# The first weights of the condition in four column steps, a selection product in place of transposes, and three projection tiles fed slice by slice

## The reference, cut to what matters

```python
def adaln(cond, w, b):
    m = jax.nn.silu(cond) @ w + b
    return jnp.split(m.reshape((-1, 1, N_MOD * D_MODEL)), N_MOD, axis=-1)
...
sh_m, sc_m, g_m, sh_f, sc_f, g_f = adaln(c, ada_w[l], ada_b[l])
csh_m, csc_m, ... = adaln(c_ctx, ada_w[l], ada_b[l])
h_ctx = modulate(rmsnorm(ctx, norm_mix_w[l]), csh_m, csc_m)   # h * (1 + scale) + shift
pc = split_in(h_ctx @ w_in[l])                                # forget gates and values of the context
h = modulate(rmsnorm(x, norm_mix_w[l]), sh_m, sc_m)
pl = split_in(h @ w_in[l])                                    # q, two forget gates, v, g, u, sv, two merge gates
```

## Time and profile before

| | us |
|---|---|
| median of 3 executions | 1562.19 (1561.62 to 1562.67) |
| the profiled execution | 1561.22 |
| its span in the profile | 1559.4 |
| busy PE, DVE, ACT | 1201.3, 562.7, 419.7 |
| share of DMA in the chain that ended last | 54% |

### The profile page before, as it was taken

How to read it: one execution, slowest core, us unless ns; L and a number is a source line. 1 busy time by engine, 2 the same in 40 slices (tenths; PEclk the granted TensorE clock), 3 DMA queues, 4 the chain that set the end, 5 groups by cost and what they waited for, 6 DMA issues and landing times.

```text
span 1559.4 us, 18602 instructions
## 1 busy us (share of the span) xinstructions
PE 1201.3 (77%) x8124; PEld 732.3 (47%) x8124; DVE 562.7 (36%) x827; ACT 419.7 (27%) x542; POOL 29.5 (2%) x36
## 2 busy tenths in 40 slices
PE   4999999997656657556656656756666899999997
PEld 1878899943311112111111111111111689999997
DVE  3788776511101101101101101101101597777566
ACT  3676656221100000000000000000000455367544
POOL 0002000000000000000000000000000000000000
PEclk9999999999888877878878878788878899999999
DMA  9546858599999999999999999999999855555551
GB/s 363 203 159 219 304 206 338 197 391 429 419 429 428 427 428 428 428 428 427 428 428 427 428 428 428 427 429 427 429 428 428 303 162 163 161 189 186 180 180 50
DMA packets 118719, 520.90 MB, mean 334 GB/s; under 512 B 7264, under 2 KB 85088, under 8 KB 90736
## 3 DMA queue, kind: packets, MB, share of 16 engines
q1 hardware_dynamic: 118496, 519.64, 83.3%
q10 hardware_dynamic: 144, 0.09, 0.0%
HBM read 518.66 MB, written 1.05 MB: 333 GB/s over the span
## 4 chain that ended last, share of the span: by engine, by line
DMA 54%; PE 33%; DVE 6%; ACT 3%; issue 2%; SPq 1%; DVEq 0%; ACTq 0%
DMA pair<-in_wu 27%; PE B L1652 14%; DMA pair<-in_wd 13%; DMA pair<-in_wg 11%; PE B L1656 7%; DMA wslot<-in_w_in 4%; PE B L2010 3%; DVE wslot_r L931 2%; PE B L2054 1%; PE B L1743 1%; PE B L1628 1%; ACT whi L506 1%; PE B L1974 1%; PE B L1949 0%; SPq L381 0%
## 5 line engine op out<-in xcount | busy, mean ns | idle before, releaser
L2010 PE MATMUL B<-pair,xs 128*32 128x512 f32 x2048 | 315.9, 745 | 203.8 <-DMA pair<-in_wu 126.3
L2010 PEld LDWEIGHTS B<-pair,xs 128*32 128x32 f32 x2048 | 63.3, 123 | 424.8 <-issue 178.3
L2054 PE MATMUL B<-pair,hidT 128*32 128x512 f32 x1008 | 166.2, 792 | 104.1 <-DMA pair<-in_wd 95.1
L2054 PEld LDWEIGHTS B<-pair,hidT 128*32 128x32 f32 x1008 | 31.9, 129 | 218.4 <-DMA pair<-in_wd 145.6
L931 DVE TENSOR_TENSOR wslot_r<-wslot,whj 128x2048 fp32r<-128x2048 f32 x52 | 118.8, 2288 | 31.4 <-ACT whj L506 31.4
L1652 PE MATMUL B<-hnh,whj 128*128 128x256 f32 x496 | 122.7, 285 | 0.4 <-ACT whj L506 0.4
L506 ACT ACTIVATE whj<-wslot 128x2048 fp32r<-128x2048 f32 x51 | 97.3, 1912 | 89.9 <-PE B L1656 84.2
L1652 PE MATMUL B<-hn_r,whj 128*128 128x256 f32 x496 | 121.5, 283 | 0.0
L1251 DVE SCALAR_TENSOR_TENSOR x<-B,mod,x 128x256 f32<-128x256 f32 x128 | 55.9, 479 | 149.5 <-PE B L1992 149.5
L1282 DVE COPY ye<-B 128x512 f32<-128x512 f32 x15 | 10.4, 692 | 273.5 <-PE B L2054 273.5
L1271 DVE TENSOR_TENSOR hid<-sgm,B 128x512 f32<-128x512 f32 x16 | 11.0, 688 | 262.7 <-PE B L2010 262.7
(11 more groups left out here) (475 smaller groups left out, 1821.0 us busy)
## 6 DMA issues: line engine op xcount, KB each, us to landing
pair<-in_wg SPq DMA_DIRECT2D x64, 2048.0 KB, 41.5
pair<-in_wu SPq DMA_DIRECT2D x64, 2048.0 KB, 40.9
pair<-in_wd SPq DMA_DIRECT2D x62, 2048.0 KB, 41.0
wslot<-in_w_in SPq DMA_DIRECT2D x58, 1024.0 KB, 5.2
aslot<-in_ada_w SPq DMA_DIRECT2D x20, 1024.0 KB, 7.4
wslot<-in_ada_w SPq DMA_DIRECT2D x4, 1024.0 KB, 9.2
wslot<-in_w_out SPq DMA_DIRECT2D x4, 1024.0 KB, 8.3
wslot<-in_wa SPq DMA_DIRECT2D x4, 1024.0 KB, 5.1
```

What stands on the lines that cost most here:

```text
L2010: mm = e.matmul(B[b][32 * j:32 * j + 32, :], XS[x // 8][:, k, 32 * (x % 8):32 * (x % 8) + 32], tile_at_page(t)[:, 512 * j:512 * j + 512], ...
L2054: mm = e.matmul(B[3 + db][32 * r:32 * r + 32, :], hidT[:, 128 * c + 32 * j:128 * c + 32 * j + 32], v2(tile_at_page(t + c // 2))[:, c % 2, ...
```

## The change

- The condition's 8 MB are loaded by columns: four steps s of 256 shift columns (t = 0) and 256 scale columns (t = 1), each 1 MB in runs of 1 KB. After a step the shift and scale of slices 2s and 2s+1 are complete.
- x is loaded first, then the identity, step 0, tile 0, ctx, step 1, tiles 1 and 2, steps 2 and 3, tiles 3 and 5.
- PE does a step as 2 x 8 products of 256 columns; slices k and k+4 share a 32-row group of the bank, so four partial sums lie in four row groups. ACT copies the bank, and a product with `sel` (a 128 x 2 matrix that adds the four groups) replaces the transposes and the adding.
- Sum and reciprocal root are made for x and for ctx apart. All slices of `HT` are now written by DVE (L547 is gone).
- The first three tiles are computed in pieces: slices 0, 1 after step 0, slices 2, 3 after step 1, and so on, interleaved with the steps.

```diff
+        step_slot = lambda s, t: (0, BASE + MORE + 1, BASE + MORE + 2, BASE + MORE + 3)[(2 * s + t) % 4]
+        def step_src(s, t):
+            c0 = 1024 * t + 256 * s
+            return a["ada_w"].rearrange("(k p) n -> p k n", p=128)[:, :, c0:c0 + 256]
...
+        first_row = tmp[2]
+        sel = ctmp[:, 48:50]
...
             e.dma_start(XX, a["x"].rearrange("(k p) t -> p k t", p=128)).then_inc(*l_x())
+            e.dma_start(ident, a["ident"]).then_inc(*l_id())
+            condition(0)
+            weights(0)
             e.dma_start(XC, a["ctx"].rearrange("(k p) t -> p k t", p=128)).then_inc(*l_c())
+            condition(1)
+            weights(1)
+            weights(2)
+            condition(2)
+            condition(3)
             weights(3)
+            e.wait_ge(*p_ada.at("step", 2, 0))
             weights(5)
+            e.wait_ge(*p_ada.at("step", 2, 1))
             e.dma_start(wtok0[:, 0:1152], a["msk"]).then_inc(*l_msk())
             for n, after in ((4, 0), (6, 1), (7, 2)):
                 e.wait_ge(*p_proj.at("tile", after))
                 weights(n)
...
+            def row(s):
+                e.wait_ge(*p_ada.at("step", s, 1))
+                if s:
+                    e.wait_ge(*p_ada.at("selected", s - 1))
+                e.activation(first_row, B[0], ACT.Copy).then_inc(*a_left("row", s))
...
+            squares(0)
+            scale_of(0)
+            row(0)
+            rounded_h(0, 0, 1)
             hi(0)
+            squares(1)
+            scale_of(1)
+            row(1)
+            rounded_h(0, 2, 3)
             hi(1)
+            rounded_h(1, 0, 1, 2, 3)
             hi(2)
+            for s in (2, 3):
+                row(s)
+                rounded_h(0, 2 * s, 2 * s + 1)
+                rounded_h(1, 2 * s, 2 * s + 1)
...
+            e.tensor_reduce(sel, ident.rearrange("p (g q) -> p q g", g=4)[:, 0:2, :], AX, ALU.add).then_inc(*v_step("sel"))
...
+            def modulation(s):
+                e.wait_ge(*p_ada.at("selected", s))
+                for r in range(2):
+                    e.tensor_tensor(o[:, :, :, r], i0[:, :, :, r], tm(vc_("ada_b", 0, 16)), ALU.add).then_inc(*v_mid("mod first", s, r))
+                e.wait_ge(*v_mid.now())
+                e.scalar_tensor_tensor(swm[:, 2 * s:2 * s + 2, :], mod[:, 8 + 2 * s:10 + 2 * s, :], 1.0, nb, ALU.add, ALU.mult).then_inc(*v_step("swm", s))
...
+            normed(0)
+            modulation(0)
+            rest_h(0, 0, 1)
+            lo(0)
+            normed(1)
+            modulation(1)
+            rest_h(0, 2, 3)
+            rest_h(1, 0, 1)
             lo(1)
+            rest_h(1, 2, 3)
             lo(2)
+            for s in (2, 3):
+                modulation(s)
+                rest_h(0, 2 * s, 2 * s + 1)
+                rest_h(1, 2 * s, 2 * s + 1)
...
+            def step(s):
+                for t in range(2):
+                    pg = step_slot(s, t)
+                    e.wait_ge(*landed[pg].at("step", s, t))
+                    for k in range(8):
+                        j = k % 4
+                        mm = e.matmul(B[0][32 * j:32 * j + 32, 256 * t:256 * t + 256], csil[:, k, :], kn8(slots[pg])[:, k, :], start=k < 4, stop=k >= 4)
+                    mm.then_inc(*p_ada("step", s, t))
+            def select(s):
+                e.wait_ge(*a_left.at("row", s))
+                for c in range(4):
+                    mm = e.matmul(B[1][:, 2 * c:2 * c + 2], first_row[:, half(c)], sel, start=True, stop=True)
+                mm.then_inc(*p_ada("selected", s))
...
+            sum_of(0)
+            step(0)
+            select(0)
+            first(0, 0, 1)
+            rests(0, 0, 1)
+            sum_of(1)
+            step(1)
+            select(1)
+            first(0, 2, 3)
+            first(1, 0, 1, 2, 3)
+            rests(0, 2, 3)
+            first(2, 0, 1)
+            rests(1, 0, 1, 2, 3)
+            first(2, 2, 3)
+            step(2)
+            rests(2, 0, 1)
+            select(2)
+            rests(2, 2, 3)
+            first(0, 4, 5)
+            first(1, 4, 5)
+            step(3)
+            rests(0, 4, 5)
+            rests(1, 4, 5)
+            first(2, 4)
+            select(3)
+            first(2, 5)
+            rests(2, 4, 5)
+            for n in range(3):
+                first(n, 6, 7)
+                rests(n, 6, 7)
```

## The result

The kernel after takes **1569.77 us** in the median of 4 runs (1568.82 to 1571.19), the kernel before 1562.43 beside it (4 runs, 1561.62 to 1562.79). The medians differ by 7.3 us (a quotient of 1.0047), where 5.7 were forecast. The profiled execution took 1569.88, its span is 1568.1; both are 8.7 longer than before. In the later experiments the median of before was 1561.49 to 1561.71, and against these the loss is 8.1 to 8.3.

What follows compares the result with a forecast made beforehand. DVE's and ACT's fixed list from q 0's clamp to the first scores was taken to bind; engine lists put the clamp at 61.1, 5.7 late: 1561.22 + 5.7 = 1566.9 profiled, 1567.9 median. Own range 1565 to 1571, overall 1559 to 1574.

Steps and rivals of the forecast that it cites:

- The time of q 0's clamp is what to forecast: From this DVE clamp to the first scores DVE and ACT have a fixed list; clamp 61.1 instead of 55.35, 5.7 later.
- Items 1 and 2: Front of the kernel: x at 6.5, sums, step 0 done at 16.0; copy, selection, modulation, roundings; tile 0's rest done at 23.2.
- Item 4: PE after step 1: 28 products at the slow clock, 6.0 us, to 38.7; tile 2's products and rests to 44.1.
- Items 5 and 6: Step 2 and the products behind it from 44.1 to 52.1; step 3, selection and DVE's last slices to 61.1.
- item 3: DVE's ctx adds, sum, root and scalings end at 30.6; step 1's modulation to 31.1, slice 2's rounding and rest to 32.7.
- the selection: PE's products with `sel` after each step: 0.6 us set, between 0.3 (loads alone) and 0.66 (today's four transposes).
- idle 5 or 6 us: Sign of being right: PE idle this long before the first scores near 120, instead of 0.70.
- The correction of 1.0 from the profiled execution to the median: The profiled 1561.22 lies 1.0 below the median, so the sum 1566.9 became 1567.9 for the median.
- The bound on the fast clock: Fast clock throughout: item 4 falls by 3.3, DVE's list binds after 1.6; q 0's clamp at 59.6, +4.2.
- clock stays at half: Rival: PE's clock slow until 52 instead of 40, 6.6 us more, 1574.5; chance 0.10.
- As meant: Rival: the loads bind, last step runs on landing at 42.5, q 0's clamp at 49.2, 6.2 earlier; 1556; chance 0.18.
- No change: Rival: something behind 61 gives the delay back, or the round costs 5.5 us instead of 8.5; 1562; chance 0.15.

Runs made afterwards that it cites:

- the delay: Kernel before with six extra DVE additions of 128x1024 right ahead of q 0's clamp, nothing of the change in it; 1570.57 us, ratio 1.0054.
- the filled wait: Kernel after with 18 unused products of 512 columns in PE's wait ahead of the first scores; 1568.66 us, ratio 1.0043.
- the clock kept up: Kernel after with six dummy float32 products of 512 columns in PE's waits in the first 34 us; 1568.07 us, ratio 1.0041.
- the one-pass selection: Kernel after with the bank's copy and the selection matrix in float32r, one pass instead of two; 1569.02 us, ratio 1.0046.
- the three lists: Kernel after with engine lists rewritten slice by slice, roundings ahead of q's sigmoids, the third also with loads reordered; 1560.54, 1558.64 and 1560.38 us.
- list 2: Kernel after with single-slice lists, tile 3's and 4's roundings ahead of q's sigmoids, loads in the same order; 1558.64 us, ratio 0.9982.
- list 3: Kernel after with single-slice lists, tile 4's rounding ahead of its sigmoid, ctx and x loaded first, half steps before tiles 1 and 2; 1560.38 us, ratio 0.9992.

## Why the prediction was right

**The bound.** "The time of q 0's clamp is what to forecast" holds in all six kernels whose scores wait for DVE and whose lists behind the clamp are those of before. The scores start 58.84 us behind it in before and after, 58.81 with the delay, 58.83 with the filled wait, 58.83 with the clock kept up, 58.85 with the one-pass selection. Where PE binds, they start 49.05 behind tile 3's first product (the three lists: 49.05, 49.05, 49.04). In every experiment that leaves the lists behind the clamp alone, the scores start at the later of these two.

**The sum, item by item.** Items 1 and 2 were right within 0.3 (step 0 complete at 15.94 against 16.0, tile 0's rest from 21.13 against 20.9). Item 4's products were 0.7 shorter than worked out, so step 2 started at 45.01 (44.1). Items 5 and 6 took 8.33 and 9.04, against 8.0 and 9.0. In all 62.38 instead of 61.1. That this is so near is in part luck, for two errors stand against many small ones.

**The path that was left out** is in item 3. The prediction said that DVE's scalings of ctx end last (30.6) and step 1's modulation stands behind them. They ended there (30.78), but the modulation waited for PE: the context's sum at 25.80, step 1 behind it for 3.38 at the slow clock, copy, selection: 32.14. The prediction's own prices for this path (the sum from 25.6, 1.1, two halves of 1.93, 0.65, 0.7) give 31.9; it was not laid out. With the slice behind it this made PE's block start at 34.26 and not 32.7, +1.56, of which 1.3 is the path.

**The term that was mis-sized** is the selection: 0.6 set, 1.05 and 0.95 measured (1.05 also where the dummies kept the clock at 1.00), with 0.3 and 0.66 as bounds. The row of four transposes was no upper bound: it reads x4, where four float32 products with 2 columns read x8. All four selections lie on the path, 0.35 to 0.45 each, 1.6 together. Terms that came out shorter gave 1.6 back (item 4 0.65, step 1 0.4, item 6 without its selection 0.35, and lesser ones), so that the 1.3 of the path is what remains.

**What was missed** is PE's clock in the wait before the scores. That PE would be "idle 5 or 6 us" was foreseen (4.68), its price of 1.7 was not. With it the profiled execution was 3.0 later than forecast, the median only 1.9 (1569.77 against 1567.9). The correction of 1.0 from the profiled execution to the median did not hold for the kernel after, whose profiled execution is 0.1 above its median; that it brought the forecast nearer is luck.

**The bound on the fast clock** looked at item 4 alone: 3.3 less, of which DVE's list takes back half, 1.6 left. With the clock full item 4 gained 0.9, and it was ACT's rounding of tile 2 that bound it. But the sum of ctx and step 1 gained 2.0, on the path that was left out, and the clamp was 3.3 late, not 4.2. Of this gain 0.84 came ahead of the dummies. The case "clock stays at half" did not come: the row from 40 to 42 reads 0.96.

The Trainium skill ("TensorE: Matmul & The Clock Gate", section "Loop structure matters more than you think") says that PE's clock falls where products stand behind long waits for a load, and stays up where they are dense. The trace agrees in kind, though the waits here are for ACT and DVE: the granted clock was 0.50 from 20 to 28 and from 34 to 40 us, behind waits of 3.45 and 2.15, and with dummies in the waits it was 1.00.

**"As meant"** failed as argued: steps 2 and 3 landed near 37.65 (where list 2, with the same order of these loads, waits for step 2's last half) and 44.4, 1 to 2 us later than worked out, and stood until 45.01 and 53.34 behind products that need the slices of the step before. With list 2 the loads do bind nearly, step 3 starting at 43.46, and even then the total is 3 us better than before and not the 6 that the rival gave: PE, with tile 3 at 62.19, binds.

**"No change"**: nothing gave the delay back before 360 us. But gains do get lost there: the load of `w_out` near 280 took 1.2 to 1.3 of the gains of two kernels (selection in one pass, clock kept up), and more where the clock fell.

## What to carry to other kernels

When a load is split so that work can start early, lay each engine's list step by step: a step that has landed is worth nothing while it stands behind products that need the round trip of the step before (8 to 9 us here). Lay out every engine's path to each meeting point, not only the one that seems longest. Then find the engine whose chain sets the next meeting point, and first try to shorten that chain: an exchange of two operations gave back 5.1 of 8.1 us here, and made the old kernel faster too. Before a difference between two traces is put down to an edit, see how much of it is there before the edit's first instruction. A gain at one point must be followed to the next load that it can run into.

## What the runs showed of the hardware

- Four float32 products of 128 x 128 stationary by 2 columns took 0.95 us at the full clock, 1.05 behind a wait, and 1.70 to 1.87 next to half steps whose eight products took 1.93 instead of 1.07. In one pass (float32r) they took 0.50 and 0.61.
- After a wait of 4.7 us before the scores, their eight float32 products (x16 in the trace) took 3.60 to 3.78 instead of 2.05; after waits of 2.00, 0.67 and 0.56 they took 2.05. Near 286 us a wait of 2.54 was followed by a granted clock of 0.83 over 10 us, one of 0.99 or 1.45 by 1.00.
- With six dummy products of 512 columns (0.9 to 1.0 us each) in the waits, the clock was 1.00 in the stretches where it was 0.50 without them. The context's sum and step 1 ran in 2.0 us less.
- The same lists reached the clamp at 61.69, 62.38 and 63.25 in three executions, by when PE's clock rose and fell in the first 45 us.
- The clock row does not always follow the durations: for list 3 it reads 1.00 from 30 to 40 us, where half steps took 1.93 and a selection 1.70, as at half clock.
- Loads of 1 KB runs moved 346 to 350 GB/s in all stretches of the kernel after between 20 and 44 us, however its engines worked beside them.
